# Softmax attentions on one Trainium2 core: block turns one event later, maxima ahead of scalings, and one maximum and one reciprocal for each event

## The reference, cut to what matters

```
# differential attention, 4 heads, head size 64 (two score maps for each head)
s = einsum(q, k) * scale;  s = where(causal, s, -1e30);  p = softmax(s)
a = p[:, :, 0] - lam * p[:, :, 1];          o = a @ v
# sparse attention, 8 heads: three branches for each head, each a softmax
o = gate0 * softmax(q kc) vc  +  gate1 * softmax(q ks) vs  +  gate2 * softmax(q kw) vw
```

## Time and profile before

| what | value |
|---|---|
| median of 3 runs | 2344.88 us (2342.53 to 2350.88) |
| the profiled execution, its own time | 2344.78 us |
| its span, first to last instruction | 2343.0 us |
| PE busy | 2250.0 us (96%) |
| DVE, ACT, POOL busy | 968.5, 825.3, 976.5 us |
| mean granted TensorE clock | 0.982 of full speed |
| mix1, from its first maximum to the first matmul of the output projection | 553.4 to 732.7 us |

### The profile page before, as it was taken

One profiled execution on the slowest core, in us unless ns is written; L12 is line 12 of the kernel. 1 busy time (PEld: TensorE's weight loads), 2 busy tenths in 40 slices (PEclk: granted clock), 3 DMA queues, 4 the chain that ended last, 5 costly groups with the idle time before them and its releaser, 6 DMA issues.

```text
span 2343.0 us, 28244 instructions
## 1 busy us (share of the span) xinstructions
PE 2250.0 (96%) x10366; PEld 1774.7 (76%) x10366; DVE 968.5 (41%) x1433; ACT 825.3 (35%) x1362; POOL 976.5 (42%) x435
## 2 busy tenths in 40 slices
PE   8999999998889899999999999999999889999997
PEld 6888887875446688888777888888877558888886
DVE  4112347356774512134675331124463563212344
ACT  4222235323664422222442342222352554222222
POOL 4444444552001554444453444444443433544442
PEclk9999999998989999999999999999999999999999
DMA  5222232331001133223222222222222102322221
GB/s 185 90 106 90 103 113 88 124 113 53 1 1 36 54 108 107 90 95 120 90 90 81 99 90 93 104 90 106 92 90 72 37 1 72 126 90 103 94 90 72
DMA packets 29800, 202.66 MB, mean 86 GB/s; under 512 B 3360, under 2 KB 4000, under 8 KB 6048
## 3 DMA queue, kind: packets, MB, share of 16 engines
q1 hardware_dynamic: 28800, 198.55, 24.1%
q10 hardware_dynamic: 928, 3.14, 0.4%
HBM read 198.54 MB, written 2.10 MB: 86 GB/s over the span
## 4 chain that ended last, share of the span: by engine, by line
PE 88%; DVE 6%; ACT 2%; issue 2%; POOL 1%; DMA 0%; DVEq 0%; SPq 0%; ACTq 0%; POOLq 0%
PE PS L945 27%; PE PS L947 26%; PE PS L946 26%; PE PS L1268 1%; PE PS L1237 1%; PE PS L1376 1%; DVE ACC L1433 1%; PE PS L1196 1%; DVE TMP L1513 1%; PE PS L1360 1%; DVE NMAX L1665 1%; POOL X L478 1%; PE PS L1388 1%; PE PS L1016 1%; PE PS L1092 0%
## 5 line engine op out<-in xcount | busy, mean ns | idle before, releaser
L453 POOL TENSOR_TENSOR WL<-RAW,WH 128x1024 fp32r<-128x1024 f32 x368 | 910.3, 2477 | 1273.3 <-ACT WH L520 1273.3
L945 PE MATMUL PS<-XH,WH 128*128 128x512 f32 (+1 forms) x2200 | 865.8, 394 | 29.3 <-DVE XL L1425 20.0
L947 PE MATMUL PS<-XH,WL 128*128 128x512 f32 (+1 forms) x2200 | 852.3, 387 | 0.0
L946 PE MATMUL PS<-XL,WH 128*128 128x512 f32 (+1 forms) x2200 | 852.0, 387 | 0.0
L520 ACT ACTIVATE WH<-RAW 128x1024 fp32r<-128x1024 f32 x368 | 388.1, 1059 | 1261.6 <-PE PS L947 1217.8
L945 PEld LDWEIGHTS PS<-XH,WH 128*128 128x128 f32 x2200 | 415.1, 189 | 125.7 <-POOL WL L453 18.5
L946 PEld LDWEIGHTS PS<-XL,WH 128*128 128x128 f32 x2200 | 415.5, 189 | 86.1 <-issue 4.1
L947 PEld LDWEIGHTS PS<-XH,WL 128*128 128x128 f32 x2200 | 414.8, 189 | 84.8
L945 PE MATMUL PS<-HH,WH 128*128 128x512 f32 x672 | 261.4, 389 | 0.0
L946 PE MATMUL PS<-HL,WH 128*128 128x512 f32 x672 | 261.4, 389 | 0.0
L947 PE MATMUL PS<-HH,WL 128*128 128x512 f32 x672 | 261.4, 389 | 0.0
(11 more groups left out here) (195 smaller groups left out, 1593.3 us busy)
## 6 DMA issues: line engine op xcount, KB each, us to landing
RAW<-wstream SPq DMA_DIRECT2D x183, 1024.0 KB, 4.8
X<-xT SPq DMA_DIRECT2D x4, 512.0 KB, 8.1
WORK<-memT ACTq DMA_DIRECT2D x2, 1024.0 KB, 5.6
outT<-WORK SPq DMA_DIRECT2D x8, 256.0 KB, 2.1
RAW<-wstream SPq DMA_DIRECT2D x2, 512.0 KB, 5.7
PB<-WORK ACTq DMA_DIRECT2D x8, 127.8 KB, 2.4
CST<-consts SPq DMA_DIRECT2D x1, 912.0 KB, 10.7
WORK<-constsb SPq DMA_DIRECT2D x1, 256.0 KB, 11.8
```

Source lines behind the costliest of these rows:

```text
L453: pool.tensor_tensor(WL[:, s, :, :].rearrange("p a b -> p (a b)"), RAW[:, s, :], WH[:, s, :, :].rearrange("p a b -> p (a b)").bitcast(F), ...
L945: pe.matmul(o, wh, xh, start=start, stop=False)
L946: pe.matmul(o, wh, xl, start=False, stop=False)
L947: return pe.matmul(o, wl, xh, start=False, stop=stop)
```

## The change

Three things are done to the softmax attentions.

1. The blocks of mix1 get their turn one step later (`+ (x["kind"] != "mem")`). On ACT the stores stay at the same step as before. On PE the transposes come one step later and go ahead of the values. The memory attentions keep their turns.
2. On DVE the maxima of event k go ahead of the scalings of event k-1. The take of a quad goes to the first event of the quad three further on (it was the last event of the quad two further on), ahead of finish_heads.
3. The two maxima of an event are one instruction over two PSUM banks, and wait for both score maps. The two reciprocals of an event are one instruction, which waits for both exponentials; then both scalings follow.

```diff
@@ attention_events
-            turns.setdefault(len(events) + (b >= half), []).append((x, b))
+            turns.setdefault(len(events) + (b >= half) + (x["kind"] != "mem"), []).append((x, b))
@@ ACT, attention
                 for k in range(len(events) + 3):
-                    for x, b in turns.get(k - 1, ()):
+                    for x, b in turns.get(k, ()):
                         store(x, b)
@@ PE, attention
-                for k in range(len(events) + 3):
+                for k in range(len(events) + 4):
                     if k < len(events):
                         scores(part, events[k]["members"])
+                    for item in turns.get(k, ()):
+                        transposes(*item)
                     for item in turns.get(k - 1, ()):
                         values(part, *item)
-                    for item in turns.get(k, ()):
-                        transposes(*item)
@@ DVE
-            def maximum(y):
-                for j in range(2 if y["kind"] == "diff" else 1):
-                    s = y["s"] + j
-                    dve.wait_ge(qk_done, s + 1)
-                    dve.tensor_reduce(NMAX[:, s:s + 1], PS[:, score_bank(y, j), 0:y["n"]], AX.X, ALU.max,
-                                      negate=True).then_inc(nmax_ready, 1)
+            def maxima(ys):
+                y = ys[0]
+                s, b = y["s"], score_bank(y)
+                dve.wait_ge(qk_done, s + 2)
+                dve.tensor_reduce(NMAX[:, s:s + 2], PS[:, b:b + 2, 0:y["n"]], AX.X, ALU.max,
+                                  negate=True).then_inc(nmax_ready, 2)
+
+            def scales(ys):
+                s = ys[0]["s"]
+                dve.wait_ge(exp_done, s + 2)
+                chain(dve.reciprocal(REC[:, s:s + 2], RSUM[:, s:s + 2]))
+                for y in ys:
+                    scale(y)
@@ DVE, scale: its own waits and reciprocals are gone
-                    dve.wait_ge(exp_done, s + 2)
-                    chain(dve.reciprocal(REC[:, s:s + 2], RSUM[:, s:s + 2]))
...
-                dve.wait_ge(exp_done, s + 1)
-                chain(dve.reciprocal(REC[:, s:s + 1], RSUM[:, s:s + 1]))
@@ DVE, mem_maxima and mem_scales
-                    for y in events[k]["members"]:
-                        maximum(y)
+                    maxima(events[k]["members"])
...
-                    for y in events[k]["members"]:
-                        scale(y)
+                    scales(events[k]["members"])
@@ DVE, attention
                 for k in range(len(events) + 1):
+                    if k < len(events):
+                        maxima(events[k]["members"])
                     if k:
-                        for y in events[k - 1]["members"]:
-                            scale(y)
-                    if k < len(events):
-                        for y in events[k]["members"]:
-                            maximum(y)
+                        scales(events[k - 1]["members"])
+                    if k < len(events) and events[k]["first"]:
                         t = events[k]["t"]
-                        if events[k]["first"] and part == "mix1":
-                            finish_heads(t)
-                        if events[k]["last"] and t >= 2 and qs[t - 2]["end"]:
-                            take(qs[t - 2])
-                for x in qs[-2:]:
+                        if t >= 3 and qs[t - 3]["end"]:
+                            take(qs[t - 3])
+                        finish_heads(t)
+                for x in qs[-3:]:
                     if x["end"]:
                         take(x)
```

## The result

The changed kernel takes 2310.39 us (median of 4 runs, 2308.57 to 2312.33) against 2344.58 us: the ratio is 0.9839, with a 95% interval of 0.9824 to 0.9855. It is 34.2 us faster. The forecast was 2321.3 us in a range of 2307 to 2340, so the direction and the range held, but the gain is 1.46 times the 23.5 us of the sum.

A forecast was written before the change was run, and what follows sets the result against it. The prediction held that in mix1 no engine is full and a DVE-ACT loop sets the pace. Savings of 8, 6, 4.5, 1.5 and 3.5 us over five stages sum to 23.5, from 2344.78 to 2321.3 us; range 2307 to 2340.

The forecast's parts named there:

- A loop through DVE and ACT sets the pace before: In mix1, maxima, exponentials, reciprocal and scalings take turns, 2.86 us for a sparse event with 512 columns; PE waits.
- Order on DVE: In mix1, maxima no longer wait for the previous event's scalings; the new loop through PE takes 2.0 us against 2.86.
- Turns: In mix1, transposes no longer wait for scalings just begun, so most of PE's 8.7 us of such waits goes.
- The stalls of tile 3: Four steps where PE waits behind finish_heads on ACT and then runs at low clock: 5 us gained.
- Fused instructions: Softmax attentions: fused maximum 1.22 us against 1.28 for the pair; single reciprocals saved in 48 sparse events, 9.6 us of DVE.
- The later first exponential: In mix1, the first exponential waits for both maps, 0.55 us later at 512 columns; cost between 0 and 17 us.
- The first rival: In mix1, the later first exponential eats most of the gain: 6.5 us left, 2338 us; chance 0.17.
- The stores' wait: Busiest mix1 steps: exponentials behind stores make 2.73 us an event, PE's 3.38 us decides; as rival 2343, no change 0.08.
- One sign of the prediction: ACT in the profile after: it would wait for PE before stores, not for maxima.
- The sum by stage: Mix1's gains: differential 8, tile 3 6, tile 0 4.5, tile 2 1.5, tile 1 and drain 3.5; sum 23.5 us.
- The floors: Mix1 stages at their fullest engine's load: 36, 33, 18, 24.7, 26 us; reaching all would give -41.6 us, 2303.
- The clock rival: In mix1, finer-cut PE work lengthens the 1.2 GHz stretches; slower, for example mix1 190 us, kernel 2355; chance 0.07.

The follow-up runs named there:

- T and O together: Later turns and maxima ahead of scalings, with single maxima and reciprocals (changed kernel without its fused instructions), against the kernel before: 2311.46 us, ratio 0.9853.
- O: Only the order on DVE changed, maxima of event k ahead of scalings of k-1, against the kernel before: 2375.16 us, ratio 1.0118.
- T: Only turns one step later with transposes ahead of values on PE, against the kernel before: 2332.34 us, ratio 0.9949.
- the repeat: The changed kernel measured once more, unaltered, against the kernel before: 2310.11 us, ratio 0.9854.
- F alone: Only the fused maxima and reciprocals, turns and orders as before, against the kernel before: 2376.55 us, ratio 1.0135.
- values first: Changed kernel with values ahead of transposes on PE: 2317.82 us, ratio to the kernel before 0.9882.
- the filling: Changed kernel with four extra 128x512 matmuls after the scores of event 1 of mix1: 2307.18 us, ratio to the kernel before 0.9839.
- F and T: Changed kernel with scalings put back ahead of maxima on DVE; fused instructions and later turns stay: 2353.75 us, ratio to the kernel before 1.0039.
- single maxima: Changed kernel with two single maxima for an event, reciprocals still fused: 2306.05 us, then 2307.48 us; ratios to the kernel before 0.9825 and 0.9845.
- exponentials first: Changed kernel with exponentials of event k ahead of the stores of step k on ACT: 2334.02 us, ratio to the kernel before 0.9946.
- single maxima and filling: Changed kernel with two single maxima for an event and four extra matmuls after event 1's scores in mix1: 2309.03 us, ratio to before 0.9844.

## Why the prediction was right or wrong, point by point

- *A loop through DVE and ACT sets the pace before.* Right. T and O together give 38.9 of the 42.6 us of mix1, and adding the fused instructions to a closed loop costs 21 to 24 us of mix1. Part of that loss, and of O's, is the clock too: 0.79 and 0.77 in mix1 against 0.84.
- *Order on DVE, "the new loop goes through PE", 2.0 us an event.* Right only with T. The prediction gives O no price of its own; it costs the parts one after the other and says nowhere that O needs T. The expectation of O alone, written from it, was a gain of 13 to 20 us; it is a loss of 30.
- *Turns: most of the 8.7 us goes.* Right, 2.8 us are left. *The stalls of tile 3, 5 us.* Right: none is left; what the four cost was not measured by itself.
- *Fused instructions: 1.22 us.* Right, 1.223. The 9.6 us of DVE saved by the reciprocals bought little: 0.6 and 1.2 us in the two stages that can be compared. The later first exponential costs 1 to 2 us of mix1, near the lower bound of the prediction (0 to 17). The first rival took the upper bound and was wrong, since the loop had opened. The Trainium skill (Perfetto Trace Analysis, Optimizing Scalar/DVE Operations) says that breaking instructions up may let work be completed sooner where the engine isn't saturated but causes bubbles elsewhere. For the maxima three pairs of profiles agree with it in mix1, by these 1 to 2 us; for the reciprocals the two stages disagree.
- *The stores' wait: 2.73 us an event, PE decides.* Right that it isn't the bound: ACT waits 16.7 us for transposes and values, never more than 1.5 us at a time. That their place ahead of the exponentials is worth 24 us was not seen. One sign of the prediction failed: that ACT waits before stores and not for maxima. It waits 18.1 us for maxima.
- *The sum by stage.* This is the step that failed, by size. The sum put 39, 36.5, 24.5, 27.4 and 28.3 us for the five stages, 155.7 in all; they took 34.3, 33.7, 20.2, 24.3 and 24.3, 136.7. The floors under them (36, 33, 18, 24.7, 26, 137.7) were nearly exact as a sum, in part by luck: one by one the stages came out 1.7 under, 0.7 and 2.2 over, 0.4 and 1.7 us under theirs. The 18 us on top, for "start-up", "cmp steps", steps that "must mesh" and half of the clock's loss, were not there. A step of slack between the engines was enough to let the fullest run nearly without a gap in the four sparse stages (PE busy 18.4 of 20.2 us at the least). There PE was also granted the full clock, so that its excess of the windows before vanished too. In the repeat this held for three of them: tile 0 had a clock of 0.85 and took 22.7 us, and mix1 138.4. In the differential stage even the floor was high. It stood above DVE's busy time in the row of before, 32.7 us, although by the prediction's own rule it should have been that or less. It counts four takes and all scalings; the 62 that start in the window after hold one take, add up to 31.4 us and overlap by 1.7.
- *The clock rival.* In mix1 it was wrong, the clock rose from 0.84 to 0.96. But the clock took 5.9 us at a place where the prediction did not look, because no line was changed there. With these 5.9 and 1.5 us of the rest the undersized 23.5 comes nearer to what was measured than mix1 deserved, and that is luck: 42.6 against 23.5 is a factor of 1.8.
- Open is why the stick-breaking stage draws 94.9 us in one execution and up to 104.9 in another. Its clock and its length go together in the profiles. Its start in the span does not: at 1855.65 us it took 97.2 us (F alone), at 1855.83 it took 104.9 (O alone). Nor is it shown how mix1's remaining 11 us of idle PE time divide between the engines.

## What to carry to other kernels

When no engine is full, look for the loop that passes from engine to engine, and cost a change to it as a whole: moving a producer back and giving its consumer a step of slack is one edit, and one half alone can lose nearly as much (O, 30 us) as the two together gain (33). With the slack in place the loads of the fullest engines were the better forecast here, 137.7 us against 136.7 measured, and the clock of a PE without gaps came back. Fusing two instructions delays the first result. In a closed loop that cost its full length (21 to 24 us of mix1); with the loop open the maxima still lost 1 to 2 us by it and the reciprocals gained about as much. And where a change is worth some us, compare the stages that it touches, and look at the clock of those that it doesn't.

## What the runs showed of the hardware that was not expected

The stick-breaking stage runs the same instructions in every kernel here but the two with extra matmuls in it. Its length in the profiled executions was 94.9 us (clock 0.98) before and with values first, 97.2 (0.96) with F alone, 97.8 (0.95) with the filling and in the changed kernel without masks, 98.2 (0.95) with O and T, 99.8 (0.93) with T alone, 100.5 to 100.8 (0.92) in the changed kernel twice, with F and T, with single maxima twice and in the kernel before without masks, 102.4 (0.90) with exponentials first, 104.7 (0.87) with single maxima and filling, 104.9 (0.87) with O alone. DVE is busy 64.6 to 64.8 us of it each time; PE's busy time goes from 78.5 to 88.5 us with the clock. A difference of 10 us, 0.4% of the kernel, can thus come from a stage that nobody touched.

The Trainium skill (TensorE: Matmul & The Clock Gate, What's actually happening) says that the number of slow matmuls varies from run to run of the same kernel. The runs here agree: in one group of 16 runs the kernel before took 2338.8 us at a mean clock of 0.986 in one and 2353.6 us at 0.977 in another, and the two profiles of single maxima have different patterns. The two profiles of the changed kernel have the same in this stage, to 0.01 of the clock, and its nine runs only spread from 2308.6 to 2312.3 us. Why some kernels spread more than others was not found.
